# HGRN2 stage of a decoder trunk: decay exponents in stacked matmuls, eight weight roundings on GpSimd, another order of the first pieces

## What is computed

```python
def hgrn2_mixer(x, w_in, w_o, g_norm, lower_bound):
    q, fz, i, g = jnp.split(x @ w_in, 4, axis=-1)
    q = jax.nn.silu(q)
    f = lower_bound + (1.0 - lower_bound) * jax.nn.sigmoid(fz)
    log_f = jnp.log(f)
    k = 1.0 - f
    o = hgrn2_chunk_scan(heads(q), heads(k), heads(i), heads(log_f))
    o = rms_norm(o, g_norm) * jax.nn.silu(g)
    return o @ w_o
```

## Time and profile before

| | us |
|---|---|
| median of 3 runs (995.01 to 995.99) | 995.65 |
| the profiled execution, its own time | 994.82 |
| its span | 993.3 |
| PE busy | 982.4 (99%) |
| DVE busy | 711.2 (72%) |
| ACT busy | 501.1 (50%) |
| POOL busy | 38.4 (4%) |

### The profile page before, as it was taken

The page is one execution under the profiler, slowest core; times in us unless marked ns, Lnnn a source line. Parts: engine busy times, 40 slices in busy tenths (PEclk is TensorE's granted clock), DMA queues, the critical chain, the costliest instruction groups (busy, mean ns, idle before and its releaser), DMA issues.

```text
span 993.3 us, 13958 instructions
## 1 busy us (share of the span) xinstructions
PE 982.4 (99%) x5116; PEld 829.9 (84%) x5116; DVE 711.2 (72%) x960; ACT 501.1 (50%) x571; POOL 38.4 (4%) x63
## 2 busy tenths in 40 slices
PE   9999999999999999999999999999999999999996
PEld 7888888888888888888888888888888888888885
DVE  5686667785879666668786666788877877565665
ACT  6663544346547544532444343358978535444430
POOL 0100000000210000000000000000001100000000
PEclk9999999999999999999999999999999999999999
DMA  8687655552756656563666464734233657656521
GB/s 296 221 285 243 210 168 193 170 194 103 251 202 235 220 175 205 172 233 122 215 214 210 164 211 168 236 111 145 85 128 125 215 174 239 214 167 210 165 101 42
DMA packets 129255, 184.72 MB, mean 186 GB/s; under 512 B 5952, under 2 KB 104784, under 8 KB 129088
## 3 DMA queue, kind: packets, MB, share of 16 engines
q1 hardware_dynamic: 126032, 173.56, 52.2%
q0 software_dynamic: 2624, 10.11, 2.9%
q10 hardware_dynamic: 560, 0.52, 0.2%
HBM read 183.13 MB, written 1.05 MB: 185 GB/s over the span
## 4 chain that ended last, share of the span: by engine, by line
PE 93%; DVE 2%; ACT 2%; DMA 1%; issue 0%; POOL 0%; DVEq 0%; SPq 0%; ACTq 0%
PE psum L1527 24%; PE psum L1501 17%; PE psum L1503 17%; PE psum L1502 17%; PE psum L1531 12%; PE psum L1975 1%; DMA raw<-in_ffn_w_in 1%; ACT w_hi L429 1%; PE psum L1496 1%; PE psum L1960 1%; PE psum L1644 1%; DVE w_lo L853 0%; PE psum L1940 0%; PE psum L1711 0%; DVE stats L893 0%
## 5 line engine op out<-in xcount | busy, mean ns | idle before, releaser
L853 DVE TENSOR_TENSOR w_lo<-raw,w_hi 128x2048 fp32r<-128x2048 f32 x161 | 367.4, 2287 | 40.7 <-ACT w_hi L429 40.1
L1527 PE MATMUL psum<-xT,w_hi 128*128 128x512 f32 x1024 | 358.5, 396 | 0.0
L429 ACT CAST w_hi<-raw 128x2048 fp32r<-128x2048 f32 x161 | 303.9, 1909 | 26.7 <-DMA raw<-in_ffn_w_in 15.6
L1531 PE MATMUL psum<-xT,w_lo 128*128 128x256 f32 x1024 | 275.7, 280 | 0.0
L1527 PEld LDWEIGHTS psum<-xT,w_hi 128*128 128x128 f32 x1024 | 190.4, 188 | 41.3
L1531 PEld LDWEIGHTS psum<-xT,w_lo 128*128 128x128 f32 x1024 | 192.9, 188 | 5.4
L944 DVE TENSOR_REDUCE ffn_tok<-psum 128x256 f32<-128x512 f32 x128 | 82.4, 686 | 152.3 <-PE psum L1527 152.3
L1501 PE MATMUL psum<-w_hi,xT 128*128 128x512 f32 x447 | 178.8, 400 | 0.8 <-DVE xT L874 0.7
L1503 PE MATMUL psum<-w_hi,xT 128*128 128x512 f32 x447 | 174.7, 391 | 0.0
L1502 PE MATMUL psum<-w_lo,xT 128*128 128x512 f32 x447 | 174.4, 390 | 0.0
L463 ACT ACTIVATE ffn_tok<-ffn_tok 128x256 f32<-128x256 f32 x64 | 26.8, 418 | 233.6 <-DVE ffn_tok L944 233.6
(11 more groups left out here) (197 smaller groups left out, 692.5 us busy)
## 6 DMA issues: line engine op xcount, KB each, us to landing
raw<-in_ffn_w_in SPq DMA_DIRECT2D x170, 512.0 KB, 4.7
raw<-in_ffn_w_out SPq DMA_DIRECT2D x88, 512.0 KB, 3.9
raw<-in_c_w_in SPq DMA_DIRECT2D x32, 512.0 KB, 4.5
raw<-in_ab_w_in SPq DMA_DIRECT2D x16, 512.0 KB, 4.8
raw<-in_ab_w_o SPq DMA_DIRECT2D x8, 512.0 KB, 3.8
raw<-in_c_w_o SPq DMA_DIRECT2D x8, 512.0 KB, 3.9
ln_gb<-in_ln_gain POOLq DMA_DIRECT2D x6, 512.0 KB, 6.5
ln_gb<-in_ln_bias POOLq DMA_DIRECT2D x6, 512.0 KB, 7.3
```

The source lines that it names most:

```text
L429: nc.scalar.copy(w_hi[:, n % RING], raw[:, slot]).then_inc(hi_ready, 1)
L853: nc.vector.tensor_tensor(w_lo[:, n % RING], raw[:, n % RAW], w_hi[:, n % RING].bitcast(F32), ALU.subtract).then_inc(lo_ready, 1)
L1527: return nc.tensor.matmul(dst, w_hi[:, slot, cs], xT_both[:, kk].rearrange("p a f -> p (a f)"), start=kk == 0, stop=kk == KB - 1)
L1531: return nc.tensor.matmul(dst[:, 0:SEQ], w_lo[:, slot, cs], xT_hi[:, kk], start=False, stop=False)
```

## The change

1. **Stacked exponents.** The hi and the lo part of the logarithms of 64 tokens now lie one above the other in 128 partitions (`decay_sums`), and `decay` holds each 64-row block twice. One product over 128 partitions gives hi plus lo. Level 0 (the full sums) keeps only 64 columns for each tile; the other half comes from level 1 and a total, in two `scalar_tensor_tensor` on DVE.
2. **Two half roundings.** For this stacking `log_decay` rounds in two instructions of 64 partitions, and `logf_split` subtracts in two.
3. **`head_exp`** is one ACT instruction for the first group in place of two.
4. **GpSimd rounds** units 4, 7, 8, 10, 11, 12, 13 and 15 of stage C, one ahead of the root of each head. ACT skips them, and waits for the one before where the next is its own.
5. **Start.** Piece 1 is loaded ahead of tile 1's x. Pieces 0 and 1 meet tile 0 before tile 1 is transposed.

```diff
+        POOL_SPLITS = (4, 7, 8, 10, 11, 12, 13, 15)
...
             def load_first(w):
                 load_x(0, 0)
+                load_piece(0, 1, w)
                 load_x(1, 0)
-                for k in range(1, PIECES):
+                for k in range(2, PIECES):
...
                 def split(j):
+                    if j in POOL_SPLITS:
+                        return
+                    if j - 1 in POOL_SPLITS:
+                        act.wait_ge(hi_ready, s0 + AHEAD + j)
                     split_hi(s0 + AHEAD + j)
...
-                nc.scalar.copy(hT_hi[:, par].rearrange("p (t f) -> p t f", t=TT), logf).then_inc(S["logf_hi"], 1)
+                for b in range(2):
+                    rs = slice(64 * b, 64 * b + 64)
+                    ins = nc.scalar.copy(decay_sums[b][rs, par].rearrange("p (t f) -> p t f", t=TT), logf[rs])
+                ins.then_inc(S["logf_hi"], 1)
...
-                nc.vector.tensor_tensor(lo, logf, hi.bitcast(F32), ALU.subtract).then_inc(S["logf_lo"], 1)
...
+                for b in range(2):
+                    both = decay_sums[b][:, g % 2].rearrange("p (t f) -> p t f", t=TT)
+                    rs, other = slice(64 * b, 64 * b + 64), slice(64 - 64 * b, 128 - 64 * b)
+                    ins = nc.vector.tensor_tensor(both[other], logf[rs], both[rs].bitcast(F32), ALU.subtract)
+                ins.then_inc(S["logf_lo"], 1)
...
+            def split_hi(n):
+
+                pool.wait_ge(raw_landed[n % RAW], 32 * (n // RAW))
+                used, value, _ = used_by[n - RING]
+                pool.wait_ge(used, value)
+                pool.wait_ge(hi_ready, n)
+                nc.gpsimd.tensor_copy(w_hi[:, n % RING], raw[:, n % RAW]).then_inc(hi_ready, 1)
...
                     for hd in range(8):
+                        if hd < len(POOL_SPLITS):
+                            split_hi(phases["C"] + AHEAD + POOL_SPLITS[hd])
                         pool.wait_ge(S["head_squares"], 2 * hd + 2)
...
                 first_xT(0, 0)
                 warm(2)
+                first_block()
+                first_piece(0, 1, 0)
                 first_xT(1, 0)
-                first_block()
+                warm(2)
                 first_piece(0, 0, 1)
-                for k in range(1, PIECES):
+                first_piece(0, 1, 1)
+                for k in range(2, PIECES):
...
-                for t in range(TT):
-                    full = decay[:, t, 0]
-                    nc.tensor.matmul(EXP_FULL[:, t], hi[:, t, hs], full, start=True, stop=False)
-                    nc.tensor.matmul(EXP_FULL[:, t], lo[:, t, hs], full, start=False, stop=True)
-                for b, (l0, l1) in enumerate(FACTORS):
+                for group, (l0, l1) in enumerate(FACTORS):
                     for t in range(TT):
-                        for a in (hi, lo):
-                            for half in range(2):
-                                rs = slice(64 * half, 64 * half + 64)
-                                ins = nc.tensor.matmul(EXP[b][:, half, :, t], a[rs, t, hs], decay[rs, t, l0:l1, rs],
-                                                       start=a is hi, stop=a is lo)
+                        for b in range(2):
+                            both = decay_sums[b][:, g % 2].rearrange("p (t f) -> p t f", t=TT)
+                            ins = nc.tensor.matmul(EXP[group][:, b, :, t], both[:, t, hs], decay[:, t, b, l0:l1],
+                                                   start=True, stop=True)
```

More of the change, by code:

```diff
@@ L772, in head_exp @@
                 act.wait_ge(S["exponents_done"], 2 * hd + 1 + b)
[L773 to L777, removed]
+                nc.scalar.activation(EXP_USED[b], EXP_USED[b], ACT.Exp).then_inc(S["decays_ready"], 1)
             def head_klT(hd):
@@ L1314, in head_factors, with upper_factors @@
+            def upper_factors(hd):
+                a = kqT[:, hd % 2]
                 dve.wait_ge(S["kqT_ready"], hd + 1)
                 dve.wait_ge(S["decays_ready"], 2 * hd + 1)
-                a = kqT[:, hd % 2]
                 if hd:
                     dve.wait_ge(S["head_done"], hd)
[L1320 to L1324, removed]
-                    for t in range(TT):
[L1326 to L1338, removed]
@@ L1353, in head_own, with level_copy, upper_scores, lower_scores @@
                 return steps[0]
[L1355 to L1373, removed]
+            def level_copy(n, written):
+                one = "p (n t j) -> p n t j"
+                dve.wait_ge(dve_step, written)
+                ins = nc.vector.copy_predicated(query_places(LEVELS[n]),
+                                                level_mask[:, n].rearrange(one, t=TT, j=LEVELS[n]),
+                                                LV[n].rearrange(one, t=TT, j=LEVELS[n]))
+                steps[0] += 1
+                ins.then_inc(dve_step, 1)
+                return steps[0]
+            def upper_scores(hd, written):
+                dve.wait_ge(S["levels_done"], 2 * hd + 1)
+                for n in range(4):
+                    written = level_copy(n, written)
+                return written
+            def lower_scores(hd, written):
+                dve.wait_ge(S["levels_done"], 2 * hd + 2)
+                for n in range(4, len(LEVELS)):
+                    written = level_copy(n, written)
+                dve.wait_ge(dve_step, written)
+                for t in range(TT):
+                    n = len(LEVELS) + t
+                    nc.vector.copy_predicated(scT[:, t], level_mask[:, n], LV[n]
+                                              ).then_inc(S["head_scores_ready"], 1)
             def head_gate(i, t, h0, h1):
@@ L1392, in _ @@
             first_xT_split(0, 0, 1)
+            split_lo_piece(0, 1)
             first_xT_split(1, 0)
-            for k in range(1, PIECES):
+            for k in range(2, PIECES):
                 split_lo_piece(0, k)
@@ L2050, in shape_constants @@
     mask += [below, below[::-1, ::-1]]
-    decay = []
-    for t, sums in enumerate(([keys_to_end] + levels, [a[::-1, ::-1] for a in [queries_from_start] + levels])):
-        for half, a in zip((None,) + LEVELS + (None, None), sums):
-            if half is None or half == P // 2:
-                decay.append(a)
-                continue
-            b, kind, j = np.arange(P) // 64, np.arange(P) // 32 % 2, np.arange(P) % 32
-            at = b * 64 + j // half * 2 * half + (kind ^ t) * half + j % half
-            decay.append(a[:, at])
-    for i, a in enumerate(decay + mask):
-        c[:, C_DECAY + i * P:C_DECAY + (i + 1) * P] = a
+    decay = np.zeros((P, TT, 2, N_DECAY, 64), np.float32)
+    for t in range(TT):
+        for n, (half, a) in enumerate(zip((None,) + LEVELS + (None, None), [ends] + levels)):
+            if n == 0 and t == 1:
+                a = (p >= f) & (f >= P // 2)
+            elif t == 1:
+                a = a[::-1, ::-1]
+            at = np.arange(P)
+            if half is not None and half < P // 2:
+                b, kind, j = at // 64, at // 32 % 2, at % 32
+                at = b * 64 + j // half * 2 * half + (kind ^ t) * half + j % half
+            for b in range(2):
+                rs = slice(64 * b, 64 * b + 64)
+                decay[:, t, b, n] = np.tile(a[rs][:, at[rs]], (2, 1))
+    c[:, C_DECAY:C_MASK] = decay.reshape(P, -1)
+    for i, a in enumerate(mask):
+        c[:, C_MASK + i * P:C_MASK + (i + 1) * P] = a
     return c
```

97 lines of the change are left out of this document (67 added, 30 removed).

## The result

The changed kernel takes 997.55 us (median of 15 runs, 996.70 to 999.35) against 995.26 for the kernel before (15 runs beside it). The ratio is 1.0023, 95% interval 1.0016 to 1.0030: slower by 2.3 us. The forecast was 996.5, its own range 994 to 998; as a change against the kernel before it was +0.9 us, and +2.3 was measured. The profiled execution took 997.26, 2.44 more than that of before; its span is 995.5.

The account below looks back on a forecast made before the run. PE was taken to bound stage C, with DVE second and tied to it. The terms -6.3 - 0.6 + 1.1 + 0.8 + 0.65 + 0.65 + 2.7 + 1.9 gave +0.9, forecast 996.5 us; 8-in-10 range 992.5 to 1000.

Parts of the forecast that it names:

- exponents: PE's exponents in stage C: eight products of 256 columns per head save 0.79 us a head, -6.3 us over eight heads.
- state of head 7: PE's wait for ACT's copy of head 7's state goes, as the rounding ahead moves to POOL: -0.6 us.
- logarithm, group 0: Ahead of head 0's exponents: half-height instructions cost twice, ACT 0.5 and DVE 0.6 us more, +1.1 us.
- heads 1 and 2 without GpSimd: PE waits for DVE before head 1's outputs (+0.8 us) and for head 2's exponents and factors (+0.65 us).
- later heads: Groups 2 and 3, scores, subtraction, exponents in the same order: one of them becomes late, +0.65 us.
- GpSimd's hold on DVE: POOL roundings of 2.2 us hold DVE's `w_lo` at units 10, 11, 13, 15 and partly 12: +2.7 us.
- start: Kernel start: tile 1's transposes come after three more products and are usable at 10.3 to 10.4 us: +1.9 us.
- What ACT gains is no gain of time: ACT's eight roundings fewer save nothing, since its next rounding waits for POOL's in four of the eight.
- Free copies: Rival: DVE does not wait for POOL, or copies fall where DVE reads PSUM; 991.8 to 993.8 us, chance 0.22.
- POOL the brake: Slower rival: POOL roundings of 3.1 us or more delay ACT, `w_lo` and scores; 999.5 to 1001.5 us, chance 0.27.
- The start is free: Rival: tile 1's transposes wait for nothing because its x lands later anyway; 994.6 to 995 us, chance 0.11.
- the likeliest case: The forecast itself for the whole kernel: 996.5 us, own range 994 to 998, chance 0.40.

Follow-up runs that it names:

- e4: Kernel before with the stacked exponents and two half roundings alone (parts 1 to 3), all roundings on ACT, old start: 994.46 us.
- e12: Kernel before with parts 1 to 3 and ACT's logarithm of group 0 ahead of unit 3's rounding; no GpSimd rounding, old start: 992.96 us.
- e10: Changed kernel with the old start, unit 7 rounded by ACT, and ACT's logarithm of group 0 ahead of unit 3's rounding: 992.29 us.
- e3: Kernel before with the eight GpSimd roundings alone (part 4): 997.96 us.
- e9: Changed kernel with the old start; GpSimd's rounding of unit 7 waits until DVE has begun group 1's last product of two SBUF tiles: 993.63 us.
- e2: Changed kernel with the start of before (part 5 undone): 996.24 us.
- e7: Kernel before with parts 1 to 3, only unit 3 rounded on GpSimd, and ACT copying head 1's state ahead of head 0's normalisation: 995.09 us.
- e1: Kernel before with the new start alone (part 5): 997.25 us.
- e5: Changed kernel with the old start and unit 7 rounded by ACT again, seven roundings on GpSimd: 994.04 us.

## Why the prediction was right in the sum and not in its parts

The forecast was 1.05 under the median, and would have been 1.4 under it but for the kernel before, whose three first runs (995.65) lay 0.4 above its later median. Its steps were mostly the right kinds of step, but several were mis-sized or misplaced, in both directions, and that the sum came out near is in part luck. Against the profiled executions (marks of the table; the last interval is 0.76 less for its exponents):

| step | forecast | measured in the trace |
|---|---|---|
| exponents | -6.3 | -6.1 |
| state of head 7 | -0.6 | -0.9 |
| logarithm, group 0 | +1.1 | +1.4 |
| heads 1 and 2 without GpSimd | +1.45 | +1.55 (e4, 1 to 2) |
| later heads | +0.65 | +2.1 (e4, 2 to 6) |
| GpSimd's hold on DVE | +2.7 | +1.8 |
| start | +1.9 | +2.4 |
| sum | +0.9 | +2.2 |

**The exponents** hold to 0.03 a head because two errors cancel: I had 1.71 and 0.92 where the timelines have 1.80 and 1.04. The chain's row gives head 1's exponents a start of 684.79, the timeline 684.54. **The logarithm** holds to 0.3: a half-height instruction costs like a full one (64x512 in 0.69 on DVE and 0.62 on ACT, starts 0.70 and 0.64 apart, where the earlier trace rows have 0.69 and 0.62 for 128x512). The pitch was larger than the 0.6 and 0.5 that I took, as two dependent halves hardly overlap.

**Heads 1 and 2** came out right by luck. I had 0.8 for outputs that wait for DVE's scores, 0.65 for head 2's exponents and factors, and nothing for head 1's factors. In e4 it is 0.67 before the levels of head 1, which wait for its factors (I had set their slack at 0.2 and did not take it from the 0.79 that PE comes earlier), 0.95 before its outputs, which wait for ACT, and nothing before head 2's exponents.

**The later heads** are the term that failed most. I priced one more logarithm and nothing for ACT. But with 0.76 less of PE in each head, PE meets ACT's copies and DVE's factors: in e4 it waits for them at 707.85 (0.30), 721.60 (0.27), 749.20 (0.30). With 0.16 more for each these are 1.35 of the 2.1; the rest is in waits that the view does not list, as 0.33 behind the transposes of 749.20. "What ACT gains is no gain of time" holds but for the term of head 7's state, which grew: e12 against e10 has 0.9 us in the traces, and that is the last interval (28.31 to 27.19) and 0.25 in head 0, less the 0.5 that unit 11 costs.

**GpSimd's hold on DVE**: the mechanism that I assumed holds in both directions. A rounding takes 1.90 (I took 2.2), and 3.45 under DVE's `w_lo`; two of DVE's instructions on two SBUF tiles take 1.98 (e3) and 2.00 beside it instead of 0.28 and 0.43. SBUF — State Buffer of the Trainium skill, section Who interferes with whom, has the rule that whoever issues first holds the shared ports for the whole instruction; these rows agree, and the scores of e9 agree with its exception for instructions with one SBUF input. GPSIMD Engine Reference of the Trainium skill, section 3.1, gave an estimate of 1.8 us (in my sum 0.8 less, not the 1 that I wrote); the trace has 1.90, and ACT takes 1.91 for the same. But the places were wrong. I named units 10, 11, 13 and 15 and, in part, 12. The rows show that unit 11 costs PE 0.5 (head 4 to 5, 12.37 against 11.89): beside it `w_lo` takes 3.20, DVE's scores are over at 740.35, and PE's outputs start at 740.45.

```profile
734.98 3.20 DVE L861 TENSOR_TENSOR w_lo<-raw,w_hi 128x2048 fp32r<-128x2048 f32 x1
...
740.45 0.46 PE L2044 MATMUL psum<-arena 128*128 128x128 f32 x2 [0.24 <-issue]
```

DVE is held beside 10 and 12 too, with no mark of it on PE's intervals, and the expensive one is unit 7, which I had at nothing: 1.57 of the 1.8. I had looked for meetings of a rounding with `w_lo`, the longest instruction, and not with the short ones of the decays, on which ACT's logarithm and with it three engines wait.

**The start** was right: products take over as predicted (10.31). The 2.4 of the table compares one execution with one. The first root of stage C stands between 641.99 and 643.10 in the eleven traces with the old start (before, e2 to e7, e9 to e12; mean 642.72), and at 644.71 and 644.79 in the two with the new one: 2.0, as e1's +2.05 in the medians. The executions differ because the first products do: before they run 0.31 apart (5.98 to 6.29), in the changed kernel 0.59 (5.40 to 5.99), and in e2 and e4, with the old start, the product that began at 7.72 before begins at 8.30 and 8.10. The distance is near the 0.57 that e3 has at a granted 0.50, but the granted clock of these windows reads 1.00 in all of them, so what slows these products stays open.

**The rivals.** *Free copies* fell with DVE's 2.00 and with e5, though its other condition, copies beside instructions that read PSUM, is what e9 makes true for unit 7. *POOL the brake* asked for a rounding of 2.8 us; it takes 1.90. *The start is free* fell with e1. That the ratio ends up 0.23% above one, beyond the 0.2 to which I put the likeliest case, does not come from the slower rival. The later heads cost 1.4 more than I had and GpSimd's hold 0.9 less; what executions at the lower clock add to the median is not shown.

The three parts do not add up in the medians: e1 has +2.05 and e2 +1.04, together +3.1, and the whole change has +2.29. In the traces they do (e1's +2.29 at the first root of stage C and e2's -0.13 within it make 2.16, against 2.10 for the whole change at the last root). The share of executions with the lower clock may explain the 0.8 between them; how it depends on the start was not tried.

## What to carry to other kernels

When a change makes the bounding engine's work cheaper, follow the freed time to the next wait in every stage of the loop. Of 6.1 us saved on PE, two exchanged lines on ACT decided 1.5. Before moving work to GpSimd, list what DVE reads from two SBUF tiles at that moment, short instructions included, and ask who waits for their results: a rounding of 1.9 us was free beside instructions that read PSUM and cost 1.6 us in the traces, and 2.3 in the medians, beside one of 0.43. And count the latency of a step from its issue: moving products ahead of transposes whose results come 2.1 us later gains nothing and exposes the latency.

## What was not expected of the hardware

- The clock fell to 1.2 GHz behind a wait of PE of 1.9 us in the middle of a busy stage (e3: granted 0.50 from 702 to 704), while the traced executions of the changed kernel and of e2 kept 2.4 GHz behind waits of the same length. Such a wait cost nearly twice its length there (some 1.5 us on top).
- GpSimd's rounding of 128x2048 costs the same as ACT's (1.90 and 1.91).
- A `TENSOR_SCALAR` on one SBUF tile with a scalar for each partition seems to be held by GpSimd as well: two of them take 1.08 at 721.19 in the changed kernel beside the rounding of 720.09, and 0.48 with none beside them (e4, 673.49).
